# Gate and up products of the feed-forward layers: from wide pairs to three matmuls a chunk, with the planes of x at equal places

## What is computed

```python
def swiglu_ffn(x, w_gu, w_down):
    gate, up = jnp.split(x @ w_gu, 2, axis=-1)
    return (jax.nn.silu(gate) * up) @ w_down
...
x = layer_norm_2(DEEPNORM_ALPHA * x + swiglu_ffn(x, ffn_w_gu[i], ffn_w_down[i]), ln_g[i, 1], ln_b[i, 1])
```

## Time and profile before

| | before |
|---|---|
| median of 3 runs | 856.22 us (856.12 to 857.07) |
| profiled execution, its own time | 855.29 us |
| its span in the trace | 853.5 us |
| TensorE busy (matmuls) | 841.4 us, 99% |
| TensorE weight loads | 749.8 us, 88% |
| VectorE busy | 630.3 us, 74% |
| ScalarE busy | 426.9 us, 50% |
| GpSimd busy | 79.5 us, 9% |
| read from HBM | 151.48 MB, 179 GB/s over the span |

### The profile page before, as it was taken

One profiled execution on the slowest core, in us unless ns is written; L12 is line 12 of the kernel. 1 busy time (PEld: TensorE's weight loads), 2 busy tenths in 40 slices (PEclk: granted clock), 3 DMA queues, 4 the chain that ended last, 5 costly groups with the idle time before them and its releaser, 6 DMA issues.

```text
span 853.5 us, 13053 instructions
## 1 busy us (share of the span) xinstructions
PE 841.4 (99%) x5390; PEld 749.8 (88%) x5390; DVE 630.3 (74%) x880; ACT 426.9 (50%) x613; POOL 79.5 (9%) x82
## 2 busy tenths in 40 slices
PE   9999999999999999999999999999999999999995
PEld 7998999998988987878888988889988888889885
DVE  6899957788686776787777764678978777778436
ACT  6646554456755863444444443256554544445320
POOL 0440100122003001020000000021101100000000
PEclk9999999999999999999999999999999999999999
DMA  9963776663357752467656555486545666565531
GB/s 286 289 182 94 210 206 185 188 182 124 116 153 230 226 173 84 140 204 240 187 184 196 189 187 192 132 274 199 171 138 157 221 190 197 183 191 193 183 115 50
DMA packets 121989, 154.46 MB, mean 181 GB/s; under 512 B 11663, under 2 KB 98090, under 8 KB 121930
## 3 DMA queue, kind: packets, MB, share of 16 engines
q1 hardware_dynamic: 119978, 148.23, 57.0%
q0 software_dynamic: 1872, 5.26, 1.8%
q10 hardware_dynamic: 80, 0.13, 0.0%
HBM read 151.48 MB, written 1.05 MB: 179 GB/s over the span
## 4 chain that ended last, share of the span: by engine, by line
PE 94%; DVE 4%; DMA 1%; issue 0%; ACT 0%; SPq 0%; DVEq 0%
PE acc L618 19%; PE acc L620 19%; PE acc L619 19%; PE acc L656 16%; PE acc L660 8%; PE acc L741 1%; PE acc L738 1%; PE acc L739 1%; DVE w_lo L1730 1%; PE misc L819 1%; PE acc L689 1%; PE misc L877 1%; DMA x<-in_x 1%; PE misc L1103 0%; PE misc L1080 0%
## 5 line engine op out<-in xcount | busy, mean ns | idle before, releaser
L1730 DVE TENSOR_TENSOR w_lo<-staged,w_hi 128x1024 fp32r<-128x1024 f32 (+1 forms) x274 | 334.0, 1240 | 129.9 <-ACT w_hi L1293 129.2
L1293 ACT CAST w_hi<-staged 128x1024 fp32r<-128x1024 f32 (+1 forms) x274 | 278.4, 1044 | 93.0 <-DMA staged<-in_ffn_w_down 44.7
L618 PE MATMUL acc<-x_parts,w_hi 128*128 128x256 f32 (+2 forms) x712 | 201.7, 283 | 0.6 <-DVE y_gated L1990 0.6
L619 PE MATMUL acc<-x_parts,w_hi 128*128 128x256 f32 (+2 forms) x712 | 198.1, 278 | 0.0
L620 PE MATMUL acc<-x_parts,w_lo 128*128 128x256 f32 (+2 forms) x712 | 198.0, 278 | 0.0
L656 PE MATMUL acc<-x_parts,w_hi 128*128 128x512 f32 x576 | 195.8, 393 | 0.0
L660 PE MATMUL acc<-x_parts,w_lo 128*128 128x256 f32 x576 | 149.5, 280 | 0.0
L618 PEld LDWEIGHTS acc<-x_parts,w_hi 128*128 128x128 f32 x712 | 133.9, 188 | 2.3 <-issue 1.0
L619 PEld LDWEIGHTS acc<-x_parts,w_hi 128*128 128x128 f32 x712 | 133.8, 188 | 0.7 <-issue 0.2
L620 PEld LDWEIGHTS acc<-x_parts,w_lo 128*128 128x128 f32 x712 | 133.8, 188 | 0.0
L656 PEld LDWEIGHTS acc<-x_parts,w_hi 128*128 128x128 f32 x576 | 103.7, 188 | 18.3
(11 more groups left out here) (395 smaller groups left out, 1252.8 us busy)
## 6 DMA issues: line engine op xcount, KB each, us to landing
staged<-in_ffn_w_gu SPq DMA_DIRECT2D x88, 512.0 KB, 3.6
staged<-in_w_in SPq DMA_DIRECT2D x58, 512.0 KB, 3.8
staged<-in_ffn_w_down SPq DMA_DIRECT2D x44, 512.0 KB, 3.3
staged<-in_gla_w_in SPq DMA_DIRECT2D x24, 512.0 KB, 4.4
staged<-in_moba_w_in SPq DMA_DIRECT2D x24, 512.0 KB, 3.9
staged<-in_w_o SPq DMA_DIRECT2D x8, 512.0 KB, 3.9
staged<-in_gla_w_out SPq DMA_DIRECT2D x8, 512.0 KB, 3.9
staged<-in_moba_w_out SPq DMA_DIRECT2D x8, 512.0 KB, 3.8
```

Source lines behind the costliest of these rows:

```text
L618: pe.matmul(dst, st_hi, mv_hi, start=start, stop=False)
L619: pe.matmul(dst, st_hi, mv_lo, start=False, stop=False)
L1293: nc.scalar.copy(hi, raw).then_inc(rounded, 1)
L1730: nc.vector.tensor_tensor(lo, raw, hi, ALU.subtract).then_inc(split, 1)
```

## The change

- `FFN_PAD`, `ffn_lo`, `low` and `LAST_H` are gone: every low plane lies at `xt_lo`, and `x_pair` reads two planes at equal places.
- Only up blocks 0 and 1 are made in wide pairs (slots 4 to 7). Slots 8 to 43, gate and up blocks 2 to 10, go through `t_stage`.
- For blocks 2 to 10 ScalarE takes the gate from PSUM and VectorE the up part; `gate_sum` and the semaphore `h_gated` are gone, and `up_sum` serves blocks 0 and 1 alone.

```diff
-LAST_H = FFN // 256 - 1
...
-FFN_PAD = 16
...
-        ffn_lo = plane(KC * PITCH + META + FFN_PAD, ROWS)
-
-        def low(tag):
-            return ffn_lo if tag in ("x2", "x4") else xt_lo
 
         def x_pair(k):
-            return bass.AP(planes, k * PITCH + META, [[2 * KC * PITCH, P], [KC * PITCH + FFN_PAD, 2], [1, ROWS]])
+            return bass.AP(planes, k * PITCH + META, [[2 * KC * PITCH, P], [KC * PITCH, 2], [1, ROWS]])
...
-        gate_sum = place("gate_sum", [2, ROWS])
...
-                                        mm = pe.matmul(dst, low(tag)[:, k, rows], w_hi[:, sl.ring(), cols], start=False,
+                                        mm = pe.matmul(dst, xt_lo[:, k, rows], w_hi[:, sl.ring(), cols], start=False,
...
-                wide_stage(FIRST[tag] + 6, COUNT[tag] - 10, OUT["up%d_1" % layer])
-                t_stage(FIRST[tag] + COUNT[tag] - 4, 4, OUT["gate%d_%d" % (layer, LAST_H)], xt_hi, ffn_lo)
+                wide_stage(FIRST[tag] + 6, 2, OUT["up%d_1" % layer])
+                t_stage(FIRST[tag] + 8, COUNT[tag] - 8, OUT["gate%d_2" % layer], xt_hi, xt_lo)
...
                         gate = "gate%d_%d" % (layer, b)
-                        if b < LAST_H:
-                            await_out(act, gate)
-                            nc.scalar.activation(h_gate[:], gate_sum[:], ACT.Silu).then_inc(s["h_gated"], 1)
-                        else:
-                            slot_done(act, tag, sl.index)
-                            copy_out(h_gate[:], out_t(gate), gate, ACT.Silu)
+                        slot_done(act, tag, sl.index)
+                        copy_out(h_gate[:], out_t(gate), gate, ACT.Silu)
                     if sl.index in (5, 7) or sl.index >= 8 and sl.index % 4 == 3:
 
-                        if b < LAST_H:
-                            act.wait_ge(s["hidden_ready"], layer * (FCH // 2 - 1) + b + 1)
+                        if b < 2:
+                            act.wait_ge(s["hidden_ready"], 2 * layer + b + 1)
                         else:
                             await_out(act, "up%d_%d" % (layer, b))
...
-                    if sl.index >= 8 and sl.index % 4 == 1 and sl.index // 4 < LAST_H:
-                        slot_done(dve, tag, sl.index)
-                        both_parts(gate_sum, "gate%d_%d" % (layer, sl.index // 4))
...
-                        wide = b < LAST_H
+                        wide = b < 2
                         if wide:
                             both_parts(up_sum, up)
-                        if b < 2:
                             await_read(dve, "gt%d_%d" % (layer, b))
-                        elif wide:
-                            dve.wait_ge(s["h_gated"], layer * (LAST_H - 2) + b - 1)
                         else:
                             await_out(dve, "gate%d_%d" % (layer, b))
...
-                    nc.gpsimd.tensor_tensor(low(tag)[:, 4 * j:4 * j + 4, 0:P], y[:, 0, j * 512:j * 512 + 512]
+                    nc.gpsimd.tensor_tensor(xt_lo[:, 4 * j:4 * j + 4, 0:P], y[:, 0, j * 512:j * 512 + 512]
```

More of the change, by code:

```diff
@@ L419, in hybrid_stack @@
             "conv_done", "cum_ready", "e_ready", "end_ready", "exp_done", "gain_loaded", "gain_scaled", "gg0_ready",
-            "gg1_ready", "gk_cleared", "gk_loaded", "glu_ready", "h_gated", "h_rounded", "hidden_ready", "h_split", "heads_done", "intra_ready",
+            "gg1_ready", "gk_cleared", "gk_loaded", "glu_ready", "h_rounded", "hidden_ready", "h_split", "heads_done", "intra_ready",
             "k_spread", "ke_ready", "ki_ready", "kr_roped", "kv_normed", "la_abs", "la_log", "m_added", "m_exp",
@@ L2136, in rest_rows @@
                 dve.wait_ge(s["x_rounded"], 5 * (int(tag[1]) - 1) + u + 1)
-                read(rest(low(tag)[:, lo:lo + n, t * P:t * P + P], bank(name)[:, 0:n * P].rearrange("p (c r) -> p c r", c=n),
+                read(rest(xt_lo[:, lo:lo + n, t * P:t * P + P], bank(name)[:, 0:n * P].rearrange("p (c r) -> p c r", c=n),
                           xt_hi[:, lo:lo + n, t * P:t * P + P]), name)
```

## The result

The changed kernel takes 859.22 us (858.20 to 859.64, 7 runs) against 856.85 us (855.83 to 857.07) of the kernel before in 7 runs: 1.0029 times as long, 95% interval 1.0018 to 1.0039. It is slower by some 2.4 us, where a gain of 5.1 us was forecast. That is about the size of rival B (+2.6 us).

What follows compares the result with a forecast made beforehand. TensorE's matmul start-to-start distances were taken as the bound; terms -3.9 and -1.2 us, the others 0, sum to -5.1 us, putting the median at 851.1 us, range 849.9 to 859.0.

Steps and rivals of the forecast that it cites:

- rival B: Gate-and-up triples behind wide pairs take the slower rhythm, 0.353 us, despite equal planes: 858.8 us; chance 0.12.
- What bounds the kernel: TensorE, busy 841.4 of 853.5 us; the wide stage is bound by start-to-start distances of matmuls, without waits.
- Step 1: Matmuls of 64 gate-and-up slots, 512 chunks: wide pairs of 347.7 ns become triples of 340.0 ns, -3.9 us.
- That a wide pair takes 348 and not 340 ns belongs to the padded plane: Gate-and-up wide stage: the shifted low plane was held to be why pairs exceed 340 ns.
- A third matmul as such costs nothing: Undisturbed stretches: a 512-column matmul takes 226.6 ns, twice the 113.3 of a 256-column one, so splitting is free.
- Rival A: Gate-and-up stage: the third matmul costs 10.4 ns a chunk, +5.3 us, 861.5 us in all; chance 0.09.
- N/2.4 + 2.5 ns: Skill page's price for each warm matmul of N columns; by it the change would cost +1.3 us.
- Step 2: The eight slots already in triples lose the pad: 64 chunks from 358.1 to 340.0 ns, -1.2 us.
- Step 3: The eight wide slots that stay get equal planes: taken as 0, bounds -0.5 and +0.7 us.
- its last sentence: Forecast fails if equal planes didn't make the earlier moba_qk triples quick, or wide pairs leave another rhythm behind them.
- Steps 4 and 5: n_first reading the moved low plane, and VectorE, ScalarE and SyncE work off the chain: 0 us each.

Runs made afterwards that it cites:

- e1: Changed kernel with slots 4 to 7 of each layer also in triples, so no wide pair is left: 850.69 us, 0.9927 of the kernel before.
- e4: Kernel before with the pad set to 0, wide pairs kept: 859.26 us, 1.0022 of the kernel before.
- e9: Changed kernel with slots 4 and 5 in triples, only slots 6 and 7 in wide pairs: 858.84 us, 1.0029 of the kernel before.
- e5: Float32 matmuls of 256 columns added between slots 7 and 8 of each layer: one in e1, 859.27 us; two in the changed kernel, 860.98 us.
- e2: Changed kernel with one additional float32 matmul of 256 columns between slots 7 and 8 of each layer: 852.36 us, 0.9946 of the kernel before.
- e6: e1 with the feed-forward layers' low plane 16 words further right: 859.39 us, 1.0022 of the kernel before.
- e7: e1 with the feed-forward layers' low plane 32 words further right: 859.34 us, 1.0025 of the kernel before.

## Why the prediction was wrong

It was wrong in sign: 851.1 forecast, 859.22 measured, just above the range of 849.9 to 859.0.

- **What bounds the kernel**: right. Every difference above is a matter of the distances of matmuls, at a granted clock of 1.00.
- **Step 1, the price of a triple, is the step that failed.** It took 0.340 us of the earlier trace rows because "the code after the change is the code of the earlier trace rows to the letter". The code is; the entry isn't. The earlier trace rows stand behind 512-column matmuls of one plane, the changed triples behind wide pairs. The term was -3.9 us and measured 512 x (353.5 - 347.7) ns = +3.0 us. With the entry of e1 the price of 0.340 is exactly right, so the forecast of 851.1 us nearly fits that kernel (850.69 us), where the eight wide slots gain too.
- **"That a wide pair takes 348 and not 340 ns belongs to the padded plane"**: wrong (e4). Without the pad it takes 352; no pair at 340 was seen.
- **"A third matmul as such costs nothing"**: right, e1. Rival A, which took the 0.358 us of the stage's own triples for the price of the third matmul, is refuted by it. In the same place the prediction quotes N/2.4 + 2.5 ns for each warm matmul from the Trainium skill (TensorE: Matmul & The Clock Gate, "Back-to-back issue gap"). The section gives that for an isolated matmul and says that in a stream of loads and matmuls both set the spacing, so the +1.3 us worked out from it was no price for this stage.
- **Step 2, the last eight slots**: right in sign, a quarter of the size. They went from 0.358 to 0.353, 64 x 4.6 ns = -0.3 us instead of -1.2.
- **Step 3, the wide slots that stay**: taken at 0, bounds -0.5 and +0.7; by the 0.352 of e4 it is 64 x 4 ns = +0.3 us. Its direct cost was small, and its effect was not: these slots hand on the slow rhythm to 288 triples in each layer (e1, e9). The prediction costed them as a term and named them as an entry only under B and in its last sentence.
- Together +3.0 - 0.3 + 0.3 = +3.0 us by the rows, beside some +3 read off the stages and +2.4 of the medians.
- **Steps 4 and 5**: right. The last eight matmuls of `n_first` take 1.83 us again, and ScalarE and VectorE wait for TensorE.
- **Rival B** was what happened, in its place, size and in both layers; it got a chance of 0.12. The prediction had a row for the pace, and its remark that the triples follow wide pairs directly "as they did in no row" was the open question of the whole sum. An operation seen at two prices, and an entry seen at none, should have had nearly even chances.

The slow slots of moba_qk come from its breaks: in the kernel after, each of them exchanges the rhythm. Its eighth and ninth slot, one line's instructions:

```profile
L611 PE MATMUL acc<-x_parts,w_hi x8: 281/281/468, 589.5 to 592.2; 128*128 128x256 f32 x8
```
```profile
L611 PE MATMUL acc<-x_parts,w_hi x8: 276/276/470, 593.0 to 595.6; 128*128 128x256 f32 x8
```

By the durations (281 slow, 276 quick) the eighth is slow and the ninth quick, the reverse of the earlier trace rows. Between them stand two float32 matmuls of 128 and 256 columns (L1202, L1203; each recorded as two), behind the ninth three transposes, and the tenth is slow again:

```profile
592.52 0.38 PE L1202 MATMUL misc<-mk,mq 128*128 128x128 f32 x2
592.74 0.60 PE L1203 MATMUL misc<-mk,mq 128*128 128x256 f32 x2
```
```profile
595.91 0.49 PE L1210 MATMUL misc<-const,mprobs 128*128 128x128 f32 x3
```
```profile
L611 PE MATMUL acc<-x_parts,w_hi x8: 281/281/363, 596.2 to 598.7; 128*128 128x256 f32 x8
```

So two matmuls of unequal width exchange the rhythm where the two of equal width of e5 did not, and an even number alone is no rule. Nor is an exchange certain: in the kernel before, the first of these breaks left the eighth slot quick, and that is why its ninth is slow.

```profile
L618 PE MATMUL acc<-x_parts,w_hi x8: 276/276/470, 587.1 to 589.7; 128*128 128x256 f32 x8
```

What stays open: what in TensorE the two rhythms are, how the place of a plane acts on them, and why one float32 matmul, three transposes or two matmuls of unequal width exchange them while two of equal width, or eight transposes, don't.

## What to carry to other kernels

Where TensorE is the bound and never waits, compare a change of form by start-to-start distances, and take the price of a form only from a stretch with the same operand places and the same predecessor. If a form is seen at two distances, look for what stood in front of each and try a break or another first block before giving the form up: here 32 wide pairs a layer (16 are enough, e9) in front of 288 triples made the difference between 859.2 and 850.7 us, 8.5 us in all. A few instructions kept in an old form "because they cost the same" can set the pace of everything behind them.

## What the runs showed of the hardware

- A stream of load and 256-column matmul in threes has lasting rhythms: 0.340 or 0.353 us a triple with planes at equal places, 0.353 or 0.358 with the low plane 64 bytes further right, at a granted clock of 1.00. A rhythm held for 36 slots, some 100 us, until the stage ended.
- One float32 matmul of 256 columns in between exchanged the rhythm both ways (e2, e5), two did not. Three transposes did (moba_qk, kernel after), eight did not (e1).
- Moving the low plane by 64 or 128 bytes went with 0.013 us more a triple (e1 against e6 and e7; directly or through the entry is open), and by 64 bytes with 0.004 us less a wide pair (e4 against before).
- With planes at equal places a recorded matmul's duration marks the rhythm: 276 ns in the quick one, 281 in the slow one.
